# PEER experts computed for every token from streamed tables instead of gathered rows

## The reference, cut to what matters

```python
def peer_ffn(h, w_q, subkeys, u_tab, v_tab):
    q = (x @ w_q).reshape(n_tok, PEER_HEADS, 2, PEER_KEY_DIM // 2)          # 8 heads, two halves of 128
    s = jnp.einsum('thpd,hpnd->thpn', q, subkeys).astype(jnp.float32)       # 128 keys in each half
    half_s, half_i = lax.top_k(s, PEER_TOPK)                                # 16 best
    cand = half_s[:, :, 0, :, None] + half_s[:, :, 1, None, :]
    best_s, best_i = lax.top_k(cand.reshape(n_tok, PEER_HEADS, PEER_TOPK * PEER_TOPK), PEER_TOPK)
    i1 = jnp.take_along_axis(half_i[:, :, 0], best_i // PEER_TOPK, axis=-1)
    i2 = jnp.take_along_axis(half_i[:, :, 1], best_i % PEER_TOPK, axis=-1)
    experts = (i1 * PEER_N_KEYS + i2)                                       # of 128 * 128 = 16384
    gates = jax.nn.softmax(best_s, axis=-1)
    act = jax.nn.gelu(jnp.einsum('td,tkd->tk', xt, jnp.take(u_tab, e, axis=0)), approximate=False) * g
    return jnp.einsum('tk,tkd->td', act, jnp.take(v_tab, e, axis=0))
```

## Time and profile before

| | |
|---|---|
| time, median of 3 runs (lowest to highest) | 3181.33 us (3174.66 to 3184.97) |
| profiled execution, span | 3182.4 us |
| TensorE matmuls busy | 2560.7 us |
| TensorE weight loads busy | 1447.1 us |
| VectorE busy | 2120.2 us |
| ScalarE busy | 733.8 us |
| GpSimd busy | 1699.9 us |
| moved by DMA | 1071 MB |

### The profile page before, as it was taken

The page is one execution under the profiler, slowest core; times in us unless marked ns, Lnnn a source line. Parts: engine busy times, 40 slices in busy tenths (PEclk is TensorE's granted clock), DMA queues, the critical chain, the costliest instruction groups (busy, mean ns, idle before and its releaser), DMA issues.

```text
span 3182.4 us, 30101 instructions
## 1 busy us (share of the span) xinstructions
PE 2560.7 (80%) x8920; PEld 1447.1 (45%) x8920; DVE 2120.2 (67%) x5267; ACT 733.8 (23%) x1870; POOL 1699.9 (53%) x1540
## 2 busy tenths in 40 slices
PE   7898876989787789989897779797987766677666
PEld 2586633757463323366552235475655222232222
DVE  4633588887679993356559645877677977656665
ACT  1121112552112221143122111345111221111111
POOL 0000065555447774445557745654444777777775
PEclk9889887989898899989999989898998999888888
DMA  8856497987889999999999979897977999999997
GB/s 334 301 189 222 148 360 300 335 308 296 296 318 343 386 384 414 414 380 402 410 415 384 370 257 361 313 333 270 347 278 257 369 352 343 356 355 415 413 414 320
DMA packets 296224, 1071.03 MB, mean 337 GB/s; under 512 B 33536, under 2 KB 36352, under 8 KB 295296
## 3 DMA queue, kind: packets, MB, share of 16 engines
q0 software_dynamic: 221184, 805.40, 66.5%
q1 hardware_dynamic: 71712, 253.16, 21.3%
q10 hardware_dynamic: 3168, 10.55, 0.9%
HBM read 1065.67 MB, written 3.31 MB: 336 GB/s over the span
## 4 chain that ended last, share of the span: by engine, by line
PE 40%; DVE 21%; POOL 16%; DMA 12%; issue 10%; ACT 1%; SPq 0%; DVEq 0%; ACTq 0%; POOLq 0%
POOL ring L1687 10%; PE psum L723 9%; PE psum L813 7%; PE psum L802 6%; POOL work L1687 6%; PE psum L972 5%; DMA ring<-in_peer_v,experts 5%; DVE ring L1241 3%; PE psum L954 3%; PE psum L838 2%; DMA ring<-in_peer_u,experts 2%; PE psum L764 2%; DMA work<-in_peer_u,experts 2%; DVE work L1339 1%; DMA wring<-in_wpack 1%
## 5 line engine op out<-in xcount | busy, mean ns | idle before, releaser
L723 PE MATMUL psum<-ring,wdiag 128*128 128x512 f32 x1688 | 903.4, 678 | 337.9 <-DMA ring<-in_peer_v,experts 204.2
L1687 POOL DMA_INDIRECT ring<-in_peer_u,experts x488 | 573.1, 1174 | 941.5 <-DVE experts L1486 412.5
L1687 POOL DMA_INDIRECT ring<-in_peer_v,experts x620 | 670.8, 1082 | 361.3 <-PE psum L723 194.5
L723 PEld LDWEIGHTS psum<-ring,wdiag 128*128 128x128 f32 x1688 | 338.8, 214 | 849.9 <-issue 496.7
L1241 DVE CUSTOM_DVE_ANT_0 work<-work 128x1024 f32<-128x1024 f32 x280 | 340.0, 1226 | 197.1 <-DMA work<-in_peer_u,experts 194.4
L1241 DVE CUSTOM_DVE_ANT_0 ring<-ring,work 128x1024 f32<-128x1024 f32 x232 | 281.1, 1224 | 161.3 <-DMA ring<-in_peer_u,experts 159.3
L1687 POOL DMA_INDIRECT work<-in_peer_u,experts x280 | 294.8, 1053 | 89.5 <-issue 84.1
L1241 DVE CUSTOM_DVE_ANT_0 ring<-ring,h2a 128x1024 f32<-128x1024 f32 x256 | 304.7, 1220 | 54.7 <-DMA ring<-in_peer_u,experts 54.0
L1006 ACT ACTIVATE acts<-dots 128x2 f32<-128x2 f32 x384 | 77.8, 203 | 1055.9 <-DVE dots L1241 967.2
L723 PE MATMUL psum<-work,wdiag 128*128 128x512 f32 x492 | 257.9, 661 | 67.6 <-DMA work<-in_peer_v,experts 49.2
L813 PE MATMUL psum<-work,wring 128*128 128x256 f32 (+1 forms) x1696 | 309.1, 341 | 0.0
(11 more groups left out here) (200 smaller groups left out, 2827.6 us busy)
## 6 DMA issues: line engine op xcount, KB each, us to landing
wring<-in_wpack SPq DMA_DIRECT2D x374, 512.0 KB, 7.2
ring<-in_wpack SPq DMA_DIRECT2D x94, 512.0 KB, 5.6
ring<-in_peer_v,experts POOLq DMA_INDIRECT x620, 6.5
ring<-in_peer_u,experts POOLq DMA_INDIRECT x488, 6.5
work<-in_peer_u,experts POOLq DMA_INDIRECT x280, 6.4
work<-in_rows ACTq DMA_DIRECT2D x4, 1024.0 KB, 7.9
work<-in_peer_v,experts POOLq DMA_INDIRECT x148, 6.3
work<-in_rpb ACTq DMA_DIRECT2D x2, 1024.0 KB, 12.6
```

The lines of the kernel that those rows point to most:

```text
L723: last = nc.tensor.matmul(psum[:, 6 + q, :], wdiag[:, SUM_NO[e] % SMALL, :], row(V_SLOT[e])[:, 512 * q:512 * (q + 1)], start=(e % KSEL == ...
L1687: pool.indirect_dma_start(row(slot), None, a[table], index).then_inc(got[slot], 16)
```

## The change

The tables are laid out anew by the host: block b of a layer is the 128 experts whose second key is b (`peer_u` transposed, D on partitions; `peer_v` with the experts on partitions), 512 KB each. In each stage's **pass** p TensorE goes through all 128 blocks. Step s of a pass is four blocks (context) or two (latent), so a bank of 512 columns: `("es", p, s)` makes x . u for all tokens (8 matmuls a block); ScalarE takes its Gelu into one of 6 buffers; VectorE multiplies with the dense gates (`gate`); `("ev", p, s)`, three steps later, multiplies with the rows of `peer_v` and adds into 2 banks a tile. The last T x 2 banks of PSUM are kept for that during a pass, all 8 are dealt out otherwise.

The dense gates are made once a tile, after its topk, by `gate_items`: the chosen first keys, second keys and gates are transposed (`gt`); for every token VectorE makes the one-hot rows of the first key (`hot`, four tokens in one operation) and GpSimd those of the second key times the gate (one tensor_scalar a token); TensorE multiplies the two (`gh`, one 128-column matmul a token, a bank for four); ScalarE and VectorE by turns copy the bank to a buffer, which GpSimd's queue writes to DRAM for 32 tokens at a time (`gst`, 2 MB). In the pass GpSimd's queue reads them back in chunks of four steps (`gr`, 1 MB). In latent stages the first tile's gate items stand between the second tile's topk pieces.

`dealt(main, other)` puts the items of a pass between the items of the following stage, in proportion to `cost`; the fourth pass has no stage beside it. The weight ring has 8 slots and carries the tables too. Gathers, dots, diagonals, `h2` and the three instructions that made the expert numbers go. The core of the diff, with "..." where lines are left out:

```diff
-W_RING = 6
+W_RING = 8
...
+PASSES = range(len(STAGES))
+BLOCKS = NKEYS
+def tokens(p):
+    return P * len(STAGES[p][1])
+def per_step(p):
+    return 512 // tokens(p)
+def steps_of(p):
+    return BLOCKS // per_step(p)
+EV_LAG = 3
+W_BUFS = 6
+CHUNK = 4
+HOT = 4
+BATCHES = P // HOT
+HOT_BUFS = 3
+HOT_LEAD = 2
+GROUP = 32
+PER_GROUP = GROUP // HOT
+GROUPS = P // GROUP
+BANKS = 8
...
+    out += [("ps", m, i, q) for q in range(4) for i in range(T)]
+    first = choice(m, 0)
+    out += first
+    made = gate_items(m, 0)
+    if T == 2:
+        second = choice(m, 1)
+        out += mixed(second, made)
+        made = gate_items(m, 1)
+    return out + made + [("gr", m, c) for c in range(2)]
+def choice(m, i):
+    return [("topk", m, i, g, n) for g in range(HEAD_GROUPS) for n in range(TOPK_PIECES)]
+def gate_items(m, i):
+    out = [("gt", m, i)] + [("hot", m, i, c) for c in range(HOT_LEAD)]
+    for c in range(BATCHES):
+        if c + HOT_LEAD < BATCHES:
+            out.append(("hot", m, i, c + HOT_LEAD))
+        out.append(("gh", m, i, c))
+        if c % PER_GROUP == 1 and c > PER_GROUP:
+            out.append(("gst", m, i, c // PER_GROUP - 1))
+    return out + [("gst", m, i, GROUPS - 1)]
...
+    return {"mod": 3.5, "modt": 0.5, "macc": 5, "hT": 1, "proj": 3.5, "norms": 12 * T, "gate": 1 * T, "sgu": 1, "tt": 1,
+            "mq": 2, "kv": 1, "mqt": 1, "mkt": 1, "s": 1.5, "pt": 1, "o": 1, "ot": 1, "br": 0.5 * T, "outs": 8, "gb": 1,
+            "mix": 4, "ln1": 9, "h2T": 2, "pq": 1 * T, "ps": 1, "topk": 1.5, "gt": 2, "gh": 1.3}.get(x[0], 0)
+def dense_items(p):
+    n, out = steps_of(p), []
+    for s in range(n + EV_LAG):
+        if s < n:
+            out.append(("es", p, s))
+            c = s // CHUNK + 1
+            if s % CHUNK == 0 and 2 <= c < n // CHUNK:
+                out.append(("gr", p, c))
+        if s >= EV_LAG:
+            out.append(("ev", p, s - EV_LAG))
+    return out
...
+def dealt(main, other):
+    total, due, n, out, since = sum(cost(x) for x in main), 0.0, 0, [], {}
+    def put(x):
+        out.append(x)
+        for s in slots_of(x):
+            for o in since:
+                since[o] += 1
+            since[s] = 0
+        for s in [s for s in since if last_item(s) == x or s[0] in ("v", "mod")]:
+            del since[s]
+    for x in main:
+        put(x)
+        due += cost(x)
+        if x[0] in ("proj", "mix") and x[3] + 1 < len(STAGES[x[1]][1]):
+            continue
+        while n < len(other) and n < len(other) * due / total and all(c + len(slots_of(other[n])) < W_RING for c in since.values()):
+            put(other[n])
             n += 1
-        out.append(n)
+    return out + other[n:]
...
+def program():
+    begin = [PLACE[("gr", 0, 1)] + 1] + [PLACE[("begin", m)] for m in (2, 3)] + [len(WORK)]
+    out = list(WORK[:begin[0]])
+    for p in PASSES:
+        main = WORK[begin[p]:begin[p + 1]] if p < 3 else []
+        out += (dealt(main, dense_items(p)) if main else dense_items(p)) + finish_items(p)
...
+                    if kind == "es":
+                        out = room(it)
+                        for j in range(per_step(m)):
+                            w = slot(("u", m, per_step(m) * it[2] + j), KD)
+                            for k in range(KD):
+                                last = nc.tensor.matmul(out[:, j * N:(j + 1) * N], w[:, k, :], VIEW[m].hT[:, k, :],
+                                                        start=(k == 0), stop=(k == KD - 1))
+                            last.then_inc(part_used if j + 1 < per_step(m) else psum_full, 1)
+                    elif kind == "ev":
+                        s = it[2]
+                        if s == 0:
+                            for before in SUMS_BEFORE[m]:
+                                emptied(before)
+                        pe.wait_ge(gated, STEP_NO[(m, s)] + 1)
+                        for j in range(per_step(m)):
+                            b = per_step(m) * s + j
+                            w = slot(("v", m, b), 1)[:, 0, :]
+                            for i in range(T):
+                                for q in range(2):
+                                    last = nc.tensor.matmul(psum[:, sum_banks(m)[2 * i + q], :],
+                                                            w_buf[:, STEP_NO[(m, s)] % W_BUFS, j * N + i * P:j * N + (i + 1) * P],
+                                                            w[:, 512 * q:512 * (q + 1)], start=(b == 0), stop=(b == BLOCKS - 1))
+                            last.then_inc(part_used, 1)
+                        if b == BLOCKS - 1:
+                            pe.wait_ge(part_used, PART_NO[("v", m, b)])
+                            pe.sem_inc(sums_ready, 1)
...
+                    elif kind == "gh":
+                        out = room(it).rearrange("p (b t) -> p t b", t=HOT)
+                        n = HOT_NO[it[1:]]
+                        pe.wait_ge(hot_first, n + 1)
+                        pe.wait_ge(hot_second, n + 1)
+                        for j in range(HOT):
+                            last = nc.tensor.matmul(out[:, j, :], hot[:, n % HOT_BUFS, 0, j, :], hot[:, n % HOT_BUFS, 1, j, :],
+                                                    start=True, stop=True)
+                        last.then_inc(psum_full, 1)
...
+                    if kind == "es":
+                        n = STEP_NO[it[1:]]
+                        if n == 0:
+                            stored_gates(act, GROUPS)
+                        if n >= W_BUFS:
+                            p, s = STEPS_IN_ORDER[n - W_BUFS]
+                            act.wait_ge(part_used, PART_NO[("v", p, per_step(p) * (s + 1) - 1)])
+                        full(act, it)
+                        taken(nc.scalar.activation(w_buf[:, n % W_BUFS, :], bank(it), ACT.Gelu))
...
+                def gate(m, s):
+                    n, c, per = STEP_NO[(m, s)], CHUNK_NO[(m, s // CHUNK)], per_step(m)
+                    evacuated(dve, ("es", m, s))
+                    if s % CHUNK == 0:
+                        dve.wait_ge(gates_in[c % 2], 16 * (c // 2 + 1))
+                    g = gate_buf[c % 2].rearrange("p (g b t) -> p b g t", b=CHUNK * per, t=GROUP)[:, s % CHUNK * per:(s % CHUNK + 1) * per, :, :]
+                    w = w_buf[:, n % W_BUFS, :].rearrange("p (b g t) -> p b g t", b=per, t=GROUP)
+                    nc.vector.tensor_tensor(w, w, g, ALU.mult).then_inc(gated, 1)
...
+                    if kind == "hot":
+                        n, t = HOT_NO[it[1:]], HOT * it[3]
+                        if it[3] == 0:
+                            evacuated(dve, ("gt", m, it[2]))
+                        if n >= HOT_BUFS:
+                            full(dve, ("gh",) + HOT_ORDER[n - HOT_BUFS])
+                        nc.vector.tensor_tensor(hot[:, n % HOT_BUFS, 0, :, :], spread(consts[:, K_IO:K_IO + P].unsqueeze(1), 1, HOT),
+                                                spread(chosen[:, 0, t:t + HOT].unsqueeze(2), 2, P), ALU.is_equal).then_inc(hot_first, 1)
...
+                for it in PROGRAM:
+                    kind, m = it[0:2]
+                    if kind == "hot":
+                        n = HOT_NO[it[1:]]
+                        if it[3] == 0:
+                            evacuated(pool, ("gt", m, it[2]))
+                        if n >= HOT_BUFS:
+                            full(pool, ("gh",) + HOT_ORDER[n - HOT_BUFS])
+                        for j in range(HOT):
+                            t = HOT * it[3] + j
+                            last = nc.gpsimd.tensor_scalar(hot[:, n % HOT_BUFS, 1, j, :], consts[:, K_IO:K_IO + P],
+                                                           chosen[:, 1, t:t + 1], chosen[:, 2, t:t + 1], ALU.is_equal, ALU.mult)
+                        last.then_inc(hot_second, 1)
+                    elif kind == "gst":
+                        i, k = it[2:]
+                        n = STORE_NO[it[1:]]
+                        all_evacuated(pool, [("gh", m, i, c) for c in range(PER_GROUP * k, PER_GROUP * (k + 1))])
+                        pool.dma_start(made[m][GROUPS * i + k], staging(m, n)).then_inc(gates_stored[n % 2], 16)
+                    elif kind == "gr":
+                        c, n = it[2], CHUNK_NO[it[1:]]
+                        if c == 0:
+                            stored_gates(pool, STORE_NO[(m, len(STAGES[m][1]) - 1, GROUPS - 1)] + 1)
+                        if c < 2 and m:
+                            pool.wait_ge(gated, STEP_NO[(m, 0)])
+                        elif c >= 2:
+                            pool.wait_ge(gated, STEP_NO[(m, CHUNK * (c - 1))])
+                        width = CHUNK * per_step(m) * GROUP
+                        src = made[m][:, :, width * c:width * (c + 1)].rearrange("g p n -> p g n")
+                        pool.dma_start(gate_buf[n % 2].rearrange("p (g n) -> p g n", n=width), src).then_inc(gates_in[n % 2], 16)
```

(31 more changed lines are left out.)

533 lines of the change are left out of this document (209 added, 324 removed).

## The result

The changed kernel takes **4590.91 us** (median; 4589.23 to 4592.23), the kernel before 3177.99 us on the same chip: a ratio of 1.4442, 95% interval 1.4406 to 1.4478. That is slower and inside the range (4260 to 4690). It is 190 us over the 4400 of the forecast and outside the 4300 to 4540 to which the forecast's own case was given; it lies between that case and the one in which GpSimd is late (4685), nearer to the latter. The experiments ran on several chips, where the kernel before takes 3181 to 3184 us, so a difference of a few us between two runs means nothing.

What follows compares the result with a forecast made beforehand. TensorE was shared with a gather stream and would become the bound: first pass at 481 us, plus 3760 us of TensorE work and 160 us idle, 4400 us; range 4260 to 4690 us.

Steps and rivals of the forecast that it cites:

- the forecast's own case: Whole kernel: TensorE becomes the bound and the rest is cover, 4400 us; 4300 to 4540 us with chance 0.67.
- The sign: Whole kernel: the change makes it slower, chance 0.99, against 0.01 for faster; 4400 us is 38% more.
- the main term: Expert work on TensorE: 2828 us of dense and gate matmuls come where 1182 us go.
- The step that carries it: TensorE matmuls: an f32 matmul is two records, 0.859 us for 512 columns and 0.432 for 256 without waits.
- Rival (5): Dense matmuls on TensorE: one record and one weight load each, 1402 in place of 2800 us, total 3000; chance 0.01.
- GpSimd's operation: Gates, second factor: 768 tensor_scalar at 0.35 us, 1.4 us a batch of four tokens, 45 us a tile.
- Rival (2): Gates: GpSimd late at 1.08 us, 93 us more in first tile, 90 in each latent stage, 4685 us; chance 0.11.
- the forecast's 3760 us of TensorE: TensorE from the first pass at 481 us: main work 960, dense 2657, gh of five tiles 143 us.
- rival (3): TensorE: lower clock, today's mean rows, with waits for a free bank as possible gaps, 4580 us; chance 0.07.
- 160 us of idle time: TensorE behind 481 us: waits for latent first tiles' topk, start of last stage, chains of attention and the tail.
- The chains of attention: TensorE's other waits behind 367 us: 155 us today, of which 90 us were kept as idle time.
- The start of the last stage: Layer norm waits for both tiles of the second pass with nothing dealt before it: 30 us of TensorE idle.

Runs made afterwards that it cites:

- e5: Changed kernel with the `ev` matmuls reading both operands cut to bf16, in one pass: 3792.74 us in a single execution.
- e6: Changed kernel with both dense matmuls, `ev` and `es`, reading operands cut to bf16: 3200.68 us, 1.0077 of the kernel before.
- e1: Changed kernel with GpSimd's one-hot operation for two of four tokens moved to VectorE: 4449.09 us, 1.3971 of the kernel before.
- e8: Changed kernel, f32, with three of four tokens' one-hots on VectorE, one on GpSimd, and ScalarE alone copying the banks out: 4409.05 us, 1.3867 of the kernel before.
- e9: Kernel before the change, with its own expert matmul reading diagonal and gathered row cut to bf16: 3139.77 us, 0.9884 of the kernel before.
- e7: Changed kernel with both dense matmuls cut to bf16, three of four one-hots on VectorE and ScalarE alone copying banks: 2940.39 us, 0.9253 of the kernel before.
- e2: Changed kernel with all of GpSimd's one-hot operations moved to VectorE: 4445.07 us, 1.3969 of the kernel before.

## Why the prediction was right, and what was off

**The sign and the main term** were right. The step that carries it, two records for an f32 matmul and a price by columns, holds to the second digit: 0.858 us for 512 columns and 0.432 for 256 in the last pass, full clock, 700.00 of 700 us busy. The converse is in e5 and e6, where one record instead of two, at about a quarter of the price, takes 798 and 1390 us out of the kernel. The forecast's own case, 4300 to 4540 us with a chance of 0.67, was missed by 51 us; what held is the sign, the main term and the wider range. Rival (5), which gave 3000 us for one record in place of two, is of the right kind though it never was at hand in f32; with operands cut to bf16 and the gates as they are it comes to 3200.

**The term that was mis-sized is GpSimd's operation.** I took 0.35 us, close to VectorE's 0.22, between bounds of 0.1 and 1.08 us; it is 0.89 us (681.3/768), and the shortest of the 768 is 0.78 us, so the 0.11 us for its body that stands beside the sum says little of its price. It enters three times:

- in the first tile, which has no cover: 107 instead of 45 us, so the first `es` starts at 549.8 instead of 481 us, 69 us later. Rival (2) had this mechanism, with 93 us for 1.08.
- as waits in the later tiles: 84.3 of the 133.2 us (the rest is the first tile's).
- as clock: the forecast's 3760 us of TensorE behind the first `es` became 3868. Only part of these 108 us is the operation's: moving half of it away takes 44 us of busy time out behind the first `es` (e1), and e8 takes 46 us. This I had not in the sum at all; I had it only as rival (3), with a cause (waits for PSUM banks) that no row of the changed kernel shows.

The sum of the differences, 69 + 108 + (172 - 160) = 189 us, closes by itself, since start, busy and idle time make up the span; it doesn't show whose they are. e8 does: nearly without the operation's cost the kernel ends at 4409 us, with 67 us less in the start, 46 in busy time and 70 in idle time. That e8 stands 9 us from my 4400 is partly luck, for in it two errors of the sum nearly cancel: busy time is 63 us over the forecast and idle time 58 us under it (102 instead of 160). My 160 us of idle time had no share for GpSimd, and without its 84.3 the changed kernel has 172.3 - 84.3 = 88 us. The chains of attention cost less than the 90 us that I kept: TensorE's largest wait in them (L1004) is 18.4 us behind the first `es`. The 63 us can be placed. Each item of e8 counted from its start to the start of the next, without waits, gives 2677 us for the dense matmuls (forecast 2657), 153 for `gh` (143) and 993 for the main work (960). So of the 53 us that main work was to gain at full clock some 20 came, at a clock of 0.99; why not more is open.

**GpSimd late, rival (2),** said 90 us in each latent stage and little in the second context stage. The gates of the last tiles show it: 35.4 us of waits for GpSimd from 1300 to 1460 us and 38.8 us from 3500 to 3700, at clocks of 0.81 and 0.82, and only 5.5 us in the context stage, which has 14 items beside its gates. The mechanism was right. Its size in the latent stages is somewhat over half, for e8 gains 116 us behind the first `es` in all, where rival (2) had 90 twice.

**The start of the last stage** was put at 30 us; L866 and L824 wait 7.6 + 5.7 us there (2560 to 2700 us). L866 waits once more, 10.3 us between 1000 and 1100 us, where the transposes of `h2` follow the layer norm behind the second stage's output product; this I had not named.

**DMA and the other engines** were costed at nothing, rightly: no wait for tables in the changed kernel, 197 GB/s in the mean. In one-pass form, 512 columns take 0.225 us a matmul (e5). The Trainium skill gives a sustained spacing of about 131 ns for a matmul of 512 columns (TensorE: Matmul & The Clock Gate, section "Back-to-back issue gap"); no stretch of e5 shows it, and the measurement decides. In the first tile, bursts of 2.05 us with pauses of 1.06 to 1.54 us between them stand beside a clock of 0.50 for 109 us. The Trainium skill (TensorE: Matmul & The Clock Gate, section "HAM oscillation — how this bites in real kernels") tells of a kernel whose clock falls in each long wait for a DMA between short bursts of matmuls. The trace agrees as far as the fall goes, which comes in the wait of 7.85 us for the topk ahead of the first batch; that the clock then stays low through much shorter pauses, the section doesn't say.

**Why the expected gain wasn't there.** The change removes 805 MB of gathers and 942 us of dots, and the gathers are what bound the old kernel at its end (e9: 600 us less on TensorE gain 42 us, and nothing in the last 628). It pays with 1.1 million more columns on the engine that was the cover. In f32 the dense products take 2657 us; at a quarter of the price they would take 664 us, an estimate. The sign of the change hangs on this factor, and after it on the gates (e6 against e7: 3200 and 2940).

## What to carry to other kernels

Before gathered rows are replaced by products over a whole table, count the columns and multiply by the spacing of this dtype's matmuls, read where the trace has no waits; the engine's busy share before says little of it, since work that fills waits is nearly free (600 us of it were worth 42 here) while work on the engine that then binds is paid in full. Where an operation that the trace doesn't have stands alone on the path, as the first tile's one-hots did, take the upper bound of its price for that place, and look for the low clock of the engine that waits for it: it costs time where this engine binds (44 us in e1), hardly any where it only waits. When the bound falls, look again at everything that its long items had covered: the same gates cost 182 us in f32 and 260 us in one pass.

## What was not expected of the hardware

- A GpSimd tensor_scalar of 128 x 128 f32 with two operations and two pointer scalars takes 0.89 us (681.3/768; median of single ones 0.79), VectorE's the same 0.28 us busy.
- Through 32 bursts of four matmuls with pauses of mostly 1.1 to 1.5 us the clock stays at the lower level for the whole 109 us (0.50), to which it had fallen before them. In e2, where VectorE makes the one-hots, it starts from the same 0.50, but 16 matmuls come first without a pause; then the pauses are 0.5 to 1.1 us, the same four take 1.13 us instead of 2.05, and the clock of the stretch (436 to 490 us) is 0.96. In the last tiles the gates' matmuls start at the upper level, behind a dense item, and last 2.05 us again after two pauses of 3.0 and 2.3 us (3615 to 3619 us), so GpSimd's pace is enough to bring the clock down. Whether in the first tile the run of 16 or the shorter pauses would lift it, no run here separates.
- Reading the upper half of each f32 word as bf16, with a stride of two for both operands, costs little that is visible: one record a matmul, 0.225 us for 512 columns, against 0.215 us for a quarter of the f32 matmul.
